# A transformer layer on one core: in the attention stage, two swaps in the order of TensorE and of ScalarE

## The reference

```python
# context queries: all 128 context keys
s = q @ k.T * scale;  p = softmax(s);  o = p @ v
# latent queries: a window of the grid, and 256 cached context keys, in one softmax
s_win = q @ k_band.T * scale + bias     # masked outside the window of 8 rows x 16 columns
s_ctx = q @ k_ctx.T * scale
p = softmax(concat(s_win, s_ctx))
o = p[win] @ v_band + p[ctx] @ v_ctx
```

## Time and profile before

| | us |
|---|---|
| median of three executions | 807.61 (804.86 to 809.38) |
| the profiled execution, whole | 814.42 |
| its span in the profile | 812.3 |
| TensorE busy | 681.7 (84%) |
| VectorE busy | 247.8 (31%) |
| ScalarE busy | 139.8 (17%) |
| attention stage, from the first `scores` to the last `values` | 236.7 to 382.5 |

### The profile page before, as it was taken

How to read it: one execution, slowest core, us unless ns; L and a number is a source line. 1 busy time by engine, 2 the same in 40 slices (tenths; PEclk the granted TensorE clock), 3 DMA queues, 4 the chain that set the end, 5 groups by cost and what they waited for, 6 DMA issues and landing times. The chain is left out here.

```text
span 812.3 us, 7123 instructions
## 1 busy us (share of the span) xinstructions
PE 681.7 (84%) x2388; PEld 367.3 (45%) x2388; DVE 247.8 (31%) x543; ACT 139.8 (17%) x333; POOL 127.8 (16%) x173
## 2 busy tenths in 40 slices
PE   4689999999969999999999951989989998989810
PEld 3344444445544665777444441444444444444300
DVE  4134551066051444432132245111111111111128
ACT  4011111101022453432000020111111111110111
POOL 3203330011029000001200001111010101010054
PEclk9879999999985999965999965899999999999965
DMA  9990733112040640320870031489999999998565
GB/s 340 351 370 6 253 122 117 56 48 103 1 157 3 249 166 1 132 79 17 320 258 27 26 128 51 156 257 318 308 339 298 324 299 347 301 325 275 174 230 209
DMA packets 82857, 153.18 MB, mean 189 GB/s; under 512 B 3756, under 2 KB 49852, under 8 KB 80144
## 3 DMA queue, kind: packets, MB, share of 16 engines
q1 hardware_dynamic: 71568, 115.91, 42.7%
q0 software_dynamic: 7392, 25.91, 8.9%
q10 hardware_dynamic: 3872, 11.03, 3.4%
HBM read 131.31 MB, written 21.53 MB: 188 GB/s over the span
## 5 line engine op out<-in xcount | busy, mean ns | idle before, releaser
L1303 PE MATMUL bank<-big,vr 128*128 128x512 f32 x320 | 143.5, 602 | 10.0 <-DMA big<-w 8.1
L1128 PE MATMUL bank<-big,hu 128*128 128x512 f32 x256 | 113.9, 602 | 4.0 <-DMA big<-w_in 4.0
L1303 PEld LDWEIGHTS bank<-big,vr 128*128 128x128 f32 x320 | 60.5, 192 | 90.5 <-issue 86.7
L1319 PE MATMUL bank<-big,vr 128*128 128x512 f32 x160 | 73.7, 603 | 19.7 <-DVE vr L1018 19.7
L1128 PEld LDWEIGHTS bank<-big,hu 128*128 128x128 f32 x256 | 48.6, 193 | 61.4 <-issue 57.3
L1258 PE MATMUL bank<-big 128*128 128x512 f32 x160 | 73.6, 621 | 0.7 <-issue 0.7
L1014 DVE TENSOR_TENSOR vr<-bank,vr 128x256 f32<-128x256 f32 x20 | 8.5, 425 | 144.9 <-ACT vr L659 135.4
L1319 PEld LDWEIGHTS bank<-big,vr 128*128 128x128 f32 x160 | 28.7, 189 | 51.9 <-issue 41.2
L1258 PEld LDWEIGHTS bank<-big 128*128 128x128 f32 x160 | 31.5, 199 | 39.9 <-issue 39.9
L433 POOL TENSOR_TENSOR small<-small 128x8 f32<-128x8 f32 (+1 forms) x15 | 21.5, 1431 | 133.8 <-DVE small L772 68.0
L1023 DVE COPY rs<-bank 128x512 f32<-128x512 f32 x20 | 13.8, 692 | 79.3 <-PE bank L1319 79.3
(11 more groups left out here) (206 smaller groups left out, 783.1 us busy)
## 6 DMA issues: line engine op xcount, KB each, us to landing
big<-w SPq DMA_DIRECT2D x60, 1024.0 KB, 8.8
big<-w_ada SPq DMA_DIRECT2D x12, 2048.0 KB, 13.5
big<-w_in SPq DMA_DIRECT2D x5, 2048.0 KB, 27.0
slot_out<-rs ACTq DMA_DIRECT2D x20, 512.0 KB, 6.4
slot_out<-zero SPq DMA_DIRECT2D x1, 5120.0 KB, 22.5
big<-w_out SPq DMA_DIRECT2D x2, 2048.0 KB, 10.3
hu<-ada_rows POOLq DMA_DIRECT2D x6, 512.0 KB, 12.1
h_rows<-vr SPq DMA_DIRECT2D x5, 512.0 KB, 2.6
```

The source lines that it names most:

```text
L1128: ins = T.matmul(bank[:], lhs, w[:, k, :], start=(k == 0), stop=(k == KD - 1))
L1303: ins = T.matmul(banks[6 + p][:], hgT[:, k, :], w13[p][:, k, :], start=(k == 0), stop=(k == KD - 1))
L1319: ins = T.matmul(banks[n][:], hidT[:, k, :], w2s[p][:, k, n * 512:(n + 1) * 512], start=(k == 0), stop=(k == 1))
```

## The change

On TensorE the two calls at the end of a round are swapped: `values(n - 1)` goes in front of `prob_T(n)`. On ScalarE the two at its start are swapped: `copy_pT(n - 1)` goes in front of `softmax(n)`. No instruction is added or removed, and VectorE's order stays.

```diff
@@ ScalarE
             for n in range(len(steps) + 2):
+                if 1 <= n <= len(steps):
+                    copy_pT(n - 1)
                 if n < len(steps):
                     softmax(n)
-                if 1 <= n <= len(steps):
-                    copy_pT(n - 1)
                 if n >= 2 and steps[n - 2][1] == HEADS - 1:
                     copy_aT(steps[n - 2][0])
@@ TensorE
                     scores(n + 1)
                 if n in ada_at:
                     ada_part(*ada_at[n])
-                prob_T(n)
                 if n:
                     values(n - 1)
+                prob_T(n)
             values(len(steps) - 1)
             att_T(TILES - 1)
```

## The result

The changed kernel takes 894.02 us (886.24 to 894.17, four runs) against 808.5 us for the kernel before (804.86 to 814.89, four runs too). The ratio is 1.1025, interval 1.0933 to 1.1117. The profiled execution took 893.97 us with a span of 891.8. The prediction, 809.2 us with a range from 799 to 821, is far off.

The account below looks back on a forecast made before the run. TensorE was taken to bound the attention stage. Vanished waits (-1.4 us), boundary waits (+1.1) and the end (+1.9) summed to +1.6 us on the median 807.61, so 809.2 us, range 799 to 821.

Parts of the forecast that it names:

- The bound: Attention stage: TensorE bounds it, and what the stage gains or loses reaches the kernel's end one for one.
- The steady rounds: Full-clock rounds: still 2.49 us of work, waits vanish, -1.15 us in tile 1 and -0.24 in tile 3.
- The third rival: All 40 rounds: more waits vanish than the gaps show, 0.1 us each, 4 us faster, 804 us; chance 0.08.
- The boundaries: Tile boundaries: values wait for the division, 0.5 us at step 17, 0.5 to 0.6 at step 33; +1.1 us.
- The end: Last steps of the stage: no scores left to hide the copies, +1.9 us, about 1.5 at full clock.
- The hand-over's lower bound: Stage end: delay from copy to values of 0.05 us, against 0.22 above; these bounds give 1.5 to 1.9 us added.
- The sum: Whole kernel: -1.4 + 1.1 + 1.9 = +1.6 us, giving 809.2 us on the median 807.61.
- The first rival: Step 17: two waits make the clock fall one boundary earlier, 12 to 16 us slower, 819 to 825 us; chance 0.2.
- The clock: Tile boundaries: short idles can make the clock swing, so the added 0.5 us waits speak against the change.
- a rise one round late: Tile 1: clock rises one round later, some 2 to 4 us, more if it misses step 9's last part.
- nothing changes: Rounds of 4.03 and 4.66 us, and half-clock tile 0: no gain or loss from the new order.

Follow-up runs that it names:

- The fourth set: Four kernels, first modulation parts 0 to 6 left out, changed order to round 19, four TensorE orders from round 20: 817.92, 824.03, 875.33 and 871.18 us.
- the fall at 293.1 us: Seen in the run with the kernel before's order on both engines up to round 10 and the changed order after: 868.46 us.
- The fall at 276.5 us in the first set: Seen in the run with the changed order on both engines up to round 10 and the kernel before's order after: 832.85 us.

## Why the prediction was wrong

**The bound: right.** TensorE bounds the stage, and what the stage loses reaches the end.

**The steady rounds: right for ScalarE's swap, too low for TensorE's.** The waits of tile 1 vanish as worked out (15.33 us for six rounds, 15.36 foretold), and so does that of tile 3 (three rounds up to the transposes of step 31 take 8.88 us with ScalarE's swap alone, 9.15 before). But ScalarE's swap alone does that. I took the same instructions in another order to cost the same. They cost 0.05 us more a round at full clock (2.54 for 2.49) and 0.1 at half (4.76 for 4.66). The third rival, that more waits would vanish, pointed the wrong way.

**The boundaries: right.** Foretold 0.5 and 0.5 to 0.6 us, measured 0.48 and 0.55 with the clock held.

**The end: right in kind, somewhat high.** Foretold +1.9 us at half clock, measured 9.6 - 8.1 = 1.5; at full clock foretold 1.5, measured 0.8. The hand-over's lower bound was the nearer one: at 451.86 ScalarE's copy ends, at 451.92 values begin.

**The sum.** For TensorE's swap at full clock I had 1.1 at the boundaries and 1.5 at the end, 2.6 us; it is 3.6. ScalarE's swap gives back 1.2 us in tile 1 and 0.3 in tile 3, where I had 1.4. So the sum was short by a microsecond, which would have left the time within the range. The first rival's time doesn't follow from its price: 12 to 16 us on 809.2 are 821 to 825, not 819 to 825, and the range to 821 held none of it.

**The clock: the step that failed.** The prediction took the clock's rise at 267 us as given. It listed a rise one round late at 2 to 4 us "and more if it misses the last part of step 9", and didn't work that out. Missing it costs the full-clock rounds of the whole stage: 70.5 us from step 10 to step 34. Two things in the argument were false. The first: that in rounds at half clock "nothing changes", so that the clock would rise as before. With TensorE's changed order it did not. In the kernel before, TensorE's matmuls ahead of it, at 266.87 us:

```profile
263.56 1.93 PE L1148 MATMUL bank<-big,norms 128*32 128x512 f32 x8
265.43 1.12 PE L1184 MATMUL bank<-ident,xt 128*128 128x128 f32 x4
266.33 0.53 PE L1206 MATMUL bank<-vr,po 128*128 128x64 f32 x2
266.79 0.71 PE L1165 MATMUL bank<-qk 64*128 64x256 f32 x2
```

Part (L1148), four transposes (L1184), values (L1206). The changed kernel at the same place, with no rise:

```profile
264.26 1.93 PE L1148 MATMUL bank<-big,norms 128*32 128x512 f32 x8
266.13 0.69 PE L1206 MATMUL bank<-vr,po 128*128 128x64 f32 x2
266.61 1.06 PE L1184 MATMUL bank<-ident,xt 128*128 128x128 f32 x4
267.60 1.22 PE L1165 MATMUL bank<-qk 64*128 64x256 f32 x2
```

The second: that the eight parts of tile 2 would bring the clock back, by which the first rival was priced at 12 to 16 us. In the old order they do, at the first of them. In the changed order they don't, as a round of tile 2 of the changed kernel shows:

```profile
341.60 1.54 PE L1206 MATMUL bank<-vr,po 128*128 128x64 f32 x6
...
343.79 1.27 PE L1184 MATMUL bank<-ident,xt 128*128 128x128 f32 x5
344.99 1.65 PE L1165 MATMUL bank<-qk 64*128 64x384 f32 x2
346.44 1.06 PE L1167 MATMUL bank<-cc,qk 64*128 64x256 f32 x2
347.42 1.94 PE L1148 MATMUL bank<-big,norms 128*32 128x512 f32 x8
349.29 1.54 PE L1206 MATMUL bank<-vr,po 128*128 128x64 f32 x6
```

Ten matmul instructions of values, 2.2 us, stand between the part and the transposes, and scores on the other side. The fourth set shows that TensorE's order decides the rise in tile 2: with the part beside the transposes (and so scores beside values), eight executions of eight have the time and the mean clock of a rise in the stage; without, none of eight.

The Trainium skill, TensorE: Matmul & The Clock Gate, section "What's actually happening", says that the clock's level is set by how busy the engine has been lately. The profile's busy share doesn't tell that quantity: it was 20.00 of 20 us between 352 and 372 us with the clock at half. The section "A second HAM failure mode: psum-queue depth-cycling", which the prediction weighed, bears on the falls: the trace agrees in one more place, the fall at 293.1 us behind two short waits; the same two waits at 281 to 284 us of the changed order with seven extra matmuls brought none. But the section speaks of idles, and the loss here came at a place without any.

**What stays open.** Why the neighbourhood matters, and whether it is that of part and transposes or that of scores and values, is not known; in a steady cycle of four the same pieces are there in both kinds of order. In tile 1, where the values between part and transposes have one block in round 8, the changed order found the rise in two of five profiles, and the order scores, values, part, transposes missed it in its one; what tells them apart, the place in time of the rounds for one, wasn't tried. So the miss in tile 1 is put down to TensorE's order by the swap alone (five profiles of five with the old order, two of five with the changed one), not by the part's neighbours. That all four timed executions of the changed kernel had a mean clock of 0.816 to 0.818 says only that none found it early. The fall at 276.5 us in the first set is not explained, nor ScalarE's one execution of 832.02 us, nor how much of ScalarE's 1.1% is order and how much is clock.

## What to carry to other kernels

Where a stage of small matmuls runs with a clock that changes its level on the way, look first for what lets it rise, and ask of every reorder what it moves away from that place; a term of half a microsecond can hide a factor of two on all that follows. Price the case in which a rise is missed over the whole stretch that now runs high, not over the next round. Where the engine had idle time ahead of the stage and at its waits, filling it with matmuls that nobody reads was worth more here (802.3 to 788.7 us) than either swap, and a swap on the engine that isn't the bound took the waits away without touching this.

## What the runs showed of the hardware that I hadn't expected

- Four orders of the same instructions, whose rounds with a part have no wait for another engine, gave two outcomes in the granted clock, 0.88 and 0.82 in the mean, in 16 executions without an exception.
- TensorE was busy for 8.00 of 8 us in window after window at 0.50 from 240 to 272 and from 328 to 368 us, and stayed there. The output projection, all 128 by 512, raised it within 4.7 us (459.97 to 464.7).
- The same instructions behind another neighbour take longer: transposes of four blocks issue in 0.87 us of loads behind values against 0.72 behind scores at half clock, and a round 0.05 to 0.1 us more.
